# Two neighbouring feed-forwards with the first inner product ahead of the norm, one weight split behind every norm, and two tiles of heads turned between the first scores of an attention

## The reference

```python
x = layer_norm(ALPHA * x + y, g, b)            # y: the stage's output, rows of 1024
def swiglu(x, w_gate, w_up, w_down):
    return (jax.nn.silu(x @ w_gate) * (x @ w_up)) @ w_down
```

```python
qa = apply_rope(rms_norm(qa, q_gain), ang_2d); ka = apply_rope(rms_norm(ka, k_gain), ang_2d)
out_a = global_gqa(qa, ka, va)
qb = apply_rope(qb, ang_1d); kb = apply_rope(kb, ang_1d)
out_b = window_gqa_sink(qb, kb, vb, sink)
```

## Time and profile before

| | us |
|---|---|
| median of three runs | 2605.53 |
| the profiled execution's own time | 2605.92 |
| its span in the trace | 2604.7 |
| PE busy | 2541.6 |
| DVE busy | 1050.2 |
| ACT busy | 819.1 |

### The profile page before, as it was taken

One profiled execution on the slowest core, in us unless ns is written; L12 is line 12 of the kernel. 1 busy time (PEld: TensorE's weight loads), 2 busy tenths in 40 slices (PEclk: granted clock), 3 DMA queues, 4 the chain that ended last, 5 costly groups with the idle time before them and its releaser, 6 DMA issues.

```text
span 2604.7 us, 40657 instructions
## 1 busy us (share of the span) xinstructions
PE 2541.6 (98%) x18155; PEld 1802.5 (69%) x18155; DVE 1050.2 (40%) x1488; ACT 819.1 (31%) x1138; POOL 143.1 (5%) x143
## 2 busy tenths in 40 slices
PE   8999999999999999999999999999999999899998
PEld 6799885444444444444448986888988988797897
DVE  5755562010101001010126458546546545655554
ACT  5444342010101101010124436444443434644432
POOL 2200120000000000000000001000000004300000
PEclk9999999999999999999999999999999999999999
DMA  7565458999999999999984543446556546264651
GB/s 256 198 211 183 160 211 332 371 361 386 377 357 375 390 377 355 379 379 365 381 292 149 193 162 114 162 134 208 192 170 205 184 162 233 86 206 147 216 182 54
DMA packets 335286, 641.51 MB, mean 246 GB/s; under 512 B 15620, under 2 KB 128432, under 8 KB 334976
## 3 DMA queue, kind: packets, MB, share of 16 engines
q1 hardware_dynamic: 330000, 618.64, 66.7%
q0 software_dynamic: 5104, 20.20, 2.3%
HBM read 637.72 MB, written 1.05 MB: 245 GB/s over the span
## 4 chain that ended last, share of the span: by engine, by line
PE 91%; DVE 5%; ACT 2%; issue 1%; DMA 0%; POOL 0%; SPq 0%; DVEq 0%
PE bank L572 17%; PE bank L574 17%; PE bank L573 17%; PE bank L1166 15%; PE bank L1180 8%; PE bank L1213 7%; PE bank L1235 4%; DVE part_lo L547 2%; PE bank L1198 1%; PE bank L966 1%; PE bank L937 1%; ACT part_hi L539 1%; PE bank L584 1%; PE bank L1152 1%; DVE x_rows L1763 1%
## 5 line engine op out<-in xcount | busy, mean ns | idle before, releaser
L547 DVE TENSOR_TENSOR part_lo<-raw,part_hi 128x2048 fp32r<-128x2048 f32 x251 | 570.9, 2295 | 277.0 <-ACT part_hi L539 276.7
L539 ACT ACTIVATE part_hi<-raw 128x2048 fp32r<-128x2048 f32 x251 | 472.4, 1908 | 21.0 <-DMA raw<-in_mem_w_kv_dram 6.9
L572 PE MATMUL bank<-x_hi,part_hi 128*128 128x256 f32 x1440 | 404.8, 281 | 0.0
L574 PE MATMUL bank<-x_hi,part_lo 128*128 128x256 f32 x1440 | 402.0, 279 | 0.0
L573 PE MATMUL bank<-x_lo,part_hi 128*128 128x256 f32 x1440 | 401.9, 279 | 0.0
L572 PEld LDWEIGHTS bank<-x_hi,part_hi 128*128 128x128 f32 x1440 | 270.3, 188 | 3.9 <-issue 1.0
L573 PEld LDWEIGHTS bank<-x_lo,part_hi 128*128 128x128 f32 x1440 | 269.6, 187 | 2.9
L574 PEld LDWEIGHTS bank<-x_hi,part_lo 128*128 128x128 f32 x1440 | 270.7, 188 | 0.0
L572 PE MATMUL bank<-part_hi,x_hi 128*128 128x512 f32 x528 | 213.8, 405 | 1.2 <-DVE part_lo L547 0.8
L1166 PE MATMUL bank<-raw,expert_in 128*64 128x512 f32 x896 | 214.1, 598 | 0.0
L1166 PE MATMUL bank<-raw_hi,expert_in 128*64 128x512 f32 x896 | 211.2, 592 | 0.0
(11 more groups left out here) (270 smaller groups left out, 3417.9 us busy)
## 6 DMA issues: line engine op xcount, KB each, us to landing
raw<-in_exp_w_gate_dram SPq DMA_DIRECT2D x112, 512.0 KB, 6.5
raw<-in_exp_w_up_dram SPq DMA_DIRECT2D x112, 512.0 KB, 7.4
raw_hi<-in_exp_w_gate_dram SPq DMA_DIRECT2D x112, 512.0 KB, 8.2
raw_hi<-in_exp_w_up_dram SPq DMA_DIRECT2D x112, 512.0 KB, 9.0
raw<-in_exp_w_down_dram SPq DMA_DIRECT2D x56, 1024.0 KB, 12.8
raw_hi<-in_exp_w_down_dram SPq DMA_DIRECT2D x56, 1024.0 KB, 14.2
raw<-in_ffn_w_gate_dram SPq DMA_DIRECT2D x110, 512.0 KB, 4.1
raw<-in_ffn_w_up_dram SPq DMA_DIRECT2D x110, 512.0 KB, 5.4
```

The lines of the kernel that those rows point to most:

```text
L539: p.nc.scalar.activation(p.part_hi[i][:, :], p.raw[i][:, :], ACT.Copy).then_inc(*self.rounded.step((name,)))
L547: p.nc.vector.tensor_tensor(p.part_lo[i][:, :], p.raw[i][:, :], p.part_hi[i][:, :].bitcast(F32), ALU.subtract).then_inc(*self.split.step(( ...
L572: nc.tensor.matmul(out, stat_hi, move_hi, start=start, stop=False, skip_group_check=True)
L574: return nc.tensor.matmul(out, stat_lo, move_hi, start=False, stop=stop, skip_group_check=True)
```

## The change

Three things change, and all follow from an order written by hand.

In every feed-forward but the last, the last of the splits behind the loop (slot 3 of the following stage) stands behind the second tile's norm instead of ahead of its sum. Between two feed-forwards (stages 7 and 8 alone) the first inner product h of the following stage stands between sum and norm instead of behind the norm; and PE turns the second rows behind up part 1 instead of ahead of it. In stage 5 the tiles (4, 5) of kind 1 are turned behind the first scores, ahead of the filler, instead of at j = 1.

```diff
@@ -372,6 +372,11 @@
     return [(0, 0), (1, 0), (0, 1), (1, 1)] + middle + [(n - 2, 0), (n - 1, 0), (n - 2, 1), (n - 1, 1)]
 
 
+def second_rows_later(p, st):
+
+    return p.stages[st - 1][0] == p.stages[st][0] == "ffn2"
+
+
 def by_tiles(q):
 
     return 2 <= q < NFF - 2
@@ -814,9 +819,11 @@
         up(p, st, k, q, part, 0)
         if k and not by_tiles(order[k - 1][0]):
             pe_ffn_turn(p, st, k - 1)
-        if k == 1 and st:
+        if k == 1 and not second_rows_later(p, st):
             pe_turn_rows(p, st - 1, 1)
         up(p, st, k, q, part, 1)
+        if k == 1 and second_rows_later(p, st):
+            pe_turn_rows(p, st - 1, 1)
         if k:
             down = pe_tile_down if by_tiles(order[k - 1][0]) else pe_ffn_down
             down(p, st, k - 1, *order[k - 1])
@@ -972,6 +979,8 @@
 
     m = len(items)
     pe_scores(p, st, heads, items[0])
+    for part in meanwhile.get("ramp", ()):
+        part()
     for j in range(m + 2):
         if j in idle:
             pe_meanwhile(p, 7, 7)
@@ -1024,7 +1033,7 @@
     pe.wait_ge(*p.s.at("heads_turned", st, 0, 5))
     pe.wait_ge(*p.s.at("proj", st, 2, 1))
     pe_attention(p, st, ab_heads(p, st), PAIRS, p.prob(g), [g["pT0"], g["pT1"]],
-                 {1: [lambda: two((4, 5))], 2: [lambda: two((0, 1))], 3: [lambda: two((2, 3))],
+                 {"ramp": [lambda: two((4, 5))], 2: [lambda: two((0, 1))], 3: [lambda: two((2, 3))],
                   7: [lambda: pe_out_early(p, st, 6, 7, g["cat_hi"], g["cat_lo"])]}, idle=(0, 1))
     pe_out_projection(p, st, 6, g["cat_hi"], g["cat_lo"], early=True)
 
@@ -1769,19 +1778,26 @@
     dve_norm(p, st, tt)
 
 
+def dve_hidden(p, st, k):
+
+    dve, nc, order = p.dve, p.nc, ffn_order()
+    dve.wait_ge(*p.s.at("silu", st, k))
+    if k >= 2 and by_tiles(order[k - 2][0]):
+        dve.wait_ge(*p.v.at("hT", st, k - 2))
+    elif k >= 2:
+        dve.wait_ge(*p.t.at("h_turned", st, k - 2))
+    nc.vector.tensor_tensor(p.h[k % 2][:, :], p.silu[k % 2][:, :], p.bank[4 + k % 2][:, FC:2 * FC], ALU.mult).then_inc(
+        *p.v.step(("h", st, k)))
+
+
 def dve_ffn(p, st):
     dve, nc = p.dve, p.nc
     order = ffn_order()
     last = len(order) - 1
     final = st + 1 == len(p.stages)
     for k, (q, tt) in enumerate(order):
-        dve.wait_ge(*p.s.at("silu", st, k))
-        if k >= 2 and by_tiles(order[k - 2][0]):
-            dve.wait_ge(*p.v.at("hT", st, k - 2))
-        elif k >= 2:
-            dve.wait_ge(*p.t.at("h_turned", st, k - 2))
-        nc.vector.tensor_tensor(p.h[k % 2][:, :], p.silu[k % 2][:, :], p.bank[4 + k % 2][:, FC:2 * FC], ALU.mult).then_inc(
-            *p.v.step(("h", st, k)))
+        if k or not second_rows_later(p, st):
+            dve_hidden(p, st, k)
         early, late = dense_splits(p, st, k)
         if not by_tiles(q):
             p.ring.subtract(*early)
@@ -1798,8 +1814,12 @@
             dve_norm(p, st, 0)
         if k == last and not final:
             dve_x(p, st + 1, 0)
-        p.ring.subtract(*late)
-    dve_rows(p, st, 1)
+        p.ring.subtract(*(late[:-1] if k == last else late))
+    dve_sum(p, st, 1)
+    if not final and second_rows_later(p, st + 1):
+        dve_hidden(p, st + 1, 0)
+    dve_norm(p, st, 1)
+    p.ring.subtract(*late[-1:])
 
 
 def dve_gla(p, st, layer):
```

## The result

The changed kernel takes 2609.95 us (median of 22 runs, 2606.65 to 2615.67), the kernel before, run beside it, 2605.7 us (median of 22, 2603.93 to 2608.56). The ratio is 1.0015 with a 95% interval of 1.001 to 1.0021: slower by 2.6 to 5.5 us. The difference of the medians is 4.25 us. The forecast was 2610.5 us, in a range of 2607.3 to 2612.8. The slowdown is real, since the interval leaves out 1, but small: 0.15%.

The account below looks back on a forecast made before the run. TensorE (PE), busy 98% of the span, was taken as the bound. Losses of 3.1 + 1.15 + 0.6 = 4.85 us gave 2610.8 from the profiled run, 2610.4 from the median; forecast 2610.5 us, range 2607.3 to 2612.8.

Parts of the forecast that it names:

- the low clock of stage 8: Behind stage 8's new wait, PE's clock halves for 3.40 us as before, costing 1.70 us.
- The three places: Behind stages 1, 4 and 8: 0.29 us wait for rows becomes 1.33 for the split; 1.04 us lost each, 3.1 together.
- The slower split beside POOL: In stage 5, the moved split overlaps POOL's small operations: 0.0 to 0.15 us once, taken as nothing.
- Passed on in full: At the three places PE's own work decides afterwards, so each 1.04 us delay reaches the total undiminished.
- Stage 8: Stage 7 into 8: h's 2.06 us wait goes, about 3.0 for the split comes, eight turns add 0.82; net +1.15 us.
- Stage 5: Attention start: the two tiles' four turns delay the second scores, nothing comes back; 0.6 us lost, bounds 0.0 and 0.7.
- the clock stays up behind the new wait in stage 8: Rival, chance 0.17: no low clock behind stage 8's new wait, 1.7 us less, 2608.8 us.
- the new waits of 1.3 us bring low spells of their own: Rival, more low spells, chance 0.17: new or shifted waits each bring 1.7 us; one gives 2612.2, two 2613.9.
- part is absorbed: Rival, chance 0.10: later waits take up the 0.6 us and one 1.04; about 2608.8 us.
- a split done before PE asks: Rival, not slower, chance 0.03: split ends by 310.43 instead of 311.70 behind stage 1; 4.0 us gained, 2601.5 us.

Follow-up runs that it names:

- e1: Kernel before with only the split of slot 3 moved behind the norm after feed-forwards (stages 1, 4, 7, 8); 2608.95 us, ratio 1.0012.
- e2: Kernel before with only stage 7 into 8 changed: h between sum and norm, second rows turned behind up part 1, splits unmoved; 2602.24 us, ratio 0.9988.
- e5: As e2, plus the last split placed between the two halves of the norm behind stages 1, 4 and 8; 2601.48 us, ratio 0.9984.
- e7: As e1, but both splits (slots 2 and 3 of the following stage) stand behind the norm; 2617.1 us, ratio 1.0047.
- e6: Changed kernel plus eight filler products, result unread, in the wait ahead of up part 1 of stage 8; 2610.17 us, ratio 1.0014 to the kernel before.
- e3: Kernel before with only stage 5's two tiles turned between first scores and filler, all seven filler products kept; 2606.03 us, ratio 1.0004.
- e4: As e3, but five filler products instead of seven behind the moved tiles; 2605.25 us, ratio 1.0 to the kernel before.

## Why the prediction was right

The mechanism held at all five places; one term, the low clock of stage 8, was put too high.

**The three places: right to 0.01 us.** Forecast 1.04 us each with a wait of 1.33, measured 1.04 each with waits of 1.27, 1.27 and 1.28. The chain was as worked out: the norm earlier by one split, the split in its place, PE's order unmoved, so that the split which stood ahead of rows that PE needs sooner now stood ahead of products that it needs 0.4 us later. e1 has the same three distances and the change's other parts left out. The slower split beside POOL, put at nothing, was nothing: these splits took 2.28 to 2.29 us, in stage 5 too.

**Passed on in full: borne out.** The places of e1 sum to 3.1 us, and its median moved by 3.4 (interval 0.8 to 5.5); those of the whole change to 4.39 against 4.25. Nothing later took up a part that these runs could show. The traces let it be followed for a while. Ahead of the first place the trace of after stands 0.29 us later (301.08 to 301.37), and 90 us behind it the same wait for rows stands 1.33 us later, which is 1.04 more. First before, then after:

```profile
403.00 0.66 PE L584 MATMUL bank<-consts,x_rows 128*128 128x128 f32 x4 [0.79 <-DVE x_rows L1763]
...
404.33 0.66 PE L589 MATMUL bank<-consts,x_rows 128*128 128x128 f32 x4 [0.79 <-DVE x_rows L1772]
```

Behind it, in the expert stage, the traces shift against each other by up to half a microsecond with no change there (e2 came to stand 0.5 us later against before, the changed kernel 0.25 earlier), so a single trace can't carry the proof through the whole program. The interval of one kernel alone doesn't exclude that a fraction of a microsecond is absorbed; that the change, e1, e2 and e5 come out near their sums, and the larger step of e7 within its forecast, stands for it.

**Stage 8: the mechanism right, the size off.** The forecast was that the wait of 2.06 us for h goes and one of about 3.0 comes for the split, that the eight turns fall on the path, and that the low clock costs as much again: +1.15 us. The wait came with 3.09 and the turns with 0.79 (1987.19 to 1987.98), against the 0.82 of the forecast. The term that was mis-sized is the lost clock, put at 1.70 us, half of the 3.40 of low clock. The product took 4.21 us, 1.31 above the 2.90 of full clock, since the low spell began inside the longer wait; e6, with the clock kept up, gives 1.29 for the same. Even before, with PE busy throughout, the spell had cost less than half its length: from the turn of h to the down product it was 5.52 us (1979.20 to 1984.72), and the same instructions take 3.92 in e6, so 1.60. With 1.31 in its place the step gives 1.15 - 0.39 = 0.76, and 0.74 was measured.

**Stage 5: forecast 0.6, measured 0.53** (0.52 alone in e3). The four turns took 0.46 us (1602.02 to 1602.48), PE came to them 0.17 us later than it had come to the filler (1.23 us behind the first scores' start, not 1.06), and the filler took 1.66 instead of 1.76. The grown wait ahead of the fourth scores showed that nothing comes back.

**The rivals.** That the clock stays up behind the new wait in stage 8 was wrong: it fell, though later than said. That the new waits of 1.3 us bring low spells of their own was wrong at all three places, in the changed kernel and in e1. That part is absorbed was not seen. The one that ended below before, a split done before PE asks, needed the split 1.3 us sooner; that it would then gain is shown by e2 for stage 8 (3.2 us, forecast 3.6 with the split ahead) and by e5 for the three places (0.40 each, where 0.28 had been the rival's price). Not taken in this rival was that the split need not stand behind the whole norm to free the rows.

## What to carry to other kernels

Moving work out of the way of one consumer is worth what the next consumer in line can wait: read on the waiting engine what its next instruction after the freed one needs, and how soon. Parts of one change can cancel: here the half that gained 3.2 us and the half that cost nothing there cost 0.7 together, so measure the parts apart, each from a fixed event to the end of its place. If an instruction is in the way of two consumers, look for the slot between them, as e5 does.

## What the runs showed of the hardware that was not expected

- The low clock comes by chance behind some waits. Behind the wait of 2.37 us in stage 9 it fell in the profiled executions of seven of the nine kernels, and not in those of after and e5; behind one of 2.29 us in stage 5 it fell in six of nine (not in e2, e3 and e7). No part of the change stands between these waits and the work behind them. The changed kernel's 22 runs of one program spread over 9 us, with no change in the order of work; the profiled executions of before and after differ by 1.5 us in stage 9 for this reason alone.
- In stage 8 a wait of 2.0 us or more was followed by the low clock in every trace that had one (2.06 before, 2.01 in e1, 3.09 after; in e3, e4 and e7 too). The waits of 1.25 to 1.30 us in the changed kernel, e1 and e6 never were.
- The low clock (granted 0.50) lasted 3.4 us each time, or twice that: 6.8 us in stage 5 of e5 and e6 and in stage 8 of e7.
- A longer wait can cost less clock than a shorter one: behind 2.06 us the spell fell on work in full and cost 1.60 us, behind 3.09 us some 0.5 of its 3.4 us had passed before PE was back, and it cost 1.31.
